# A copy on ScalarE and a normalisation on VectorE change places in the first attention branch of a fused two-block transformer kernel

## The reference

```python
sc = jnp.einsum('bhcqd,bhckd->bhcqk', qblk, kt).astype(jnp.float32) * scale
p = jax.nn.softmax(sc, axis=-1)
w = p[:, :, 0] - lam * p[:, :, 1]
return jnp.einsum('bhqk,bhkd->bhqd', w.astype(vt.dtype), vt)
...
oa = (rms_norm(oa, subln_g_a[l]) * (1.0 - lam_init)).reshape(b, s, WIDTH_A)
```

## Time and profile before

| what | value |
|---|---|
| three runs | 4124.42, 4115.85, 4124.31 us |
| the profiled execution | 4120.0 us, span 4118.3 us |
| mean granted TensorE clock | 0.953 |
| PE, DVE, ACT busy | 89%, 64%, 38% of the span |
| branch A, layer 0 | 157 to 441 us of the span |
| branch A, layer 1 | 1243 to 1514 us of the span |

### The profile page before, as it was taken

How to read it: one execution, slowest core, us unless ns; L and a number is a source line. 1 busy time by engine, 2 the same in 40 slices (tenths; PEclk the granted TensorE clock), 3 DMA queues, 4 the chain that set the end, 5 groups by cost and what they waited for, 6 DMA issues and landing times. The chain is left out here.

```text
span 4118.3 us, 50129 instructions
## 1 busy us (share of the span) xinstructions
PE 3655.4 (89%) x17647; PEld 3038.4 (74%) x17647; DVE 2632.1 (64%) x5013; ACT 1553.7 (38%) x2760; POOL 607.0 (15%) x508
## 2 busy tenths in 40 slices
PE   3887899999888888998997988987887999999998
PEld 2656787788766677777785845667887888888887
DVE  6766424577666653247775655559996767777777
ACT  3344434332234443433223433432286333333332
POOL 2100000101030000011011200043300223322222
PEclk8999999999999999999998988999998999999999
DMA  6332122355221112224451200022346788888887
GB/s 245 108 96 67 35 77 82 114 192 207 79 82 42 54 31 67 72 86 160 175 202 64 75 6 6 12 95 90 94 177 261 279 306 294 314 294 302 298 307 267
DMA packets 180822, 598.68 MB, mean 145 GB/s; under 512 B 18944, under 2 KB 55552, under 8 KB 177280
## 3 DMA queue, kind: packets, MB, share of 16 engines
q1 hardware_dynamic: 129488, 409.78, 28.1%
q0 software_dynamic: 51120, 186.14, 12.9%
HBM read 559.15 MB, written 36.70 MB: 145 GB/s over the span
## 5 line engine op out<-in xcount | busy, mean ns | idle before, releaser
L389 PE MATMUL ps<-mix_w,mix_h 128*128 128x384 f32 (+1 forms) x2304 | 537.1, 383 | 55.7 <-DVE mix_h L1103 22.7
L3189 PE MATMUL ps<-peer_v,peer_coef 128*128 128x512 f32 x2304 | 544.7, 392 | 26.8 <-DVE peer_coef L3304 15.8
L389 PEld LDWEIGHTS ps<-mix_w,mix_h 128*128 128x128 f32 x2304 | 424.7, 196 | 160.7 <-issue 51.0
L3189 PEld LDWEIGHTS ps<-peer_v,peer_coef 128*128 128x128 f32 x2304 | 431.9, 188 | 116.9 <-issue 16.0
L3178 PE MATMUL ps<-peer_h,peer_u 128*128 128x384 f32 x2208 | 401.1, 336 | 3.7 <-PEq L102 3.7
L3178 PEld LDWEIGHTS ps<-peer_h,peer_u 128*128 128x128 f32 x2208 | 389.0, 188 | 10.9 <-issue 4.0
L1259 PE MATMUL ps<-mlp_coef,mlp_v 128*128 128x512 f32 x1536 | 354.0, 391 | 24.4 <-DVEq L1375 24.4
L1259 PEld LDWEIGHTS ps<-mlp_coef,mlp_v 128*128 128x128 f32 x1536 | 290.3, 189 | 85.7 <-DVEq L1375 25.3
L1248 PE MATMUL ps<-mix_h,mlp_u 128*128 128x512 f32 x1344 | 310.6, 392 | 18.3 <-DVEq L1364 18.3
L1248 PEld LDWEIGHTS ps<-mix_h,mlp_u 128*128 128x128 f32 x1344 | 253.9, 189 | 72.7 <-DVEq L1364 19.5
L823 DVE TENSOR_TENSOR mix_w<-mix_raw,mix_w 128x1024 fp32r<-128x1024 f32 (+1 forms) x136 | 153.3, 1143 | 238.7 <-ACT mix_w L612 238.7
(11 more groups left out here) (553 smaller groups left out, 6551.7 us busy)
## 6 DMA issues: line engine op xcount, KB each, us to landing
peer_raw_v<-in_v_tiles SPq DMA_DIRECT2D x128, 512.0 KB, 10.2
peer_raw_u<-in_u_tiles SPq DMA_DIRECT2D x104, 512.0 KB, 11.6
mlp_tiles<-in_w_ada POOLq DMA_DIRECT2D x96, 512.0 KB, 4.6
mix_raw<-in_w_rest SPq DMA_DIRECT2D x68, 512.0 KB, 3.6
mlp_raw_v<-in_w_down SPq DMA_DIRECT2D x16, 2048.0 KB, 8.1
mlp_raw_u<-in_w_up SPq DMA_DIRECT2D x56, 512.0 KB, 9.3
mix_raw<-in_w_a SPq DMA_DIRECT2D x48, 512.0 KB, 3.7
expert_weights<-peer_table SPq DMA_DIRECT2D x6, 4096.0 KB, 12.3
```

Source lines behind the costliest of these rows:

```text
L389: last = pe.matmul(proj(u, n_cols), M.H[:, x, k, b * P:(b + 1) * P], V.w[:, y, i % SLOTS_W, k % 2 * n_cols:(k % 2 + 1) * n_cols], start=k ...
L3189: last = pe.matmul(bank(M.ps, 2 * b + half), Q.coef[:, x, t % 4, b * P:(b + 1) * P], Q.v[:, y, t % 4, half * BANK:(half + 1) * BANK], star ...
```

## The change

There are three edits. On ScalarE `a_back(n)`, the copy of the transposed weights, moves from the end of the even half to the place directly behind the exponentials, ahead of `a_post`, `unit_root` and `high`. On VectorE `head_norm` moves from the end of the odd half j = 33 + 8h to the end of the next even half, j = 34 + 8h: behind that half's maximum, sums, low parts and rope, and ahead of the next `a_weigh`. In `a_values` TensorE now waits for the output block of the step before to be taken, where it waited for the one four steps before; `a_post(n - 1)`, which itself waits for that block, used to stand ahead of the copy that the values wait for.

```diff
--- before.py
+++ after.py
@@ -447,8 +447,8 @@
             def a_values(n):
 
                 h, b = a_step(n)
-                if n >= 4:
-                    pe.wait_ge(o_taken, n - 3)
+                if n:
+                    pe.wait_ge(o_taken, n)
                 if n % 16 == 0:
                     pe.wait_ge(freed_even, (12 * (n // 16) + 12) // 2)
                     pe.wait_ge(freed_odd, (12 * (n // 16) + 12) // 2)
@@ -763,6 +763,7 @@
                             a_exp(0)
                         if n + 1 < A_STEPS:
                             a_exp(n + 1)
+                        a_back(n)
                     if in_b:
                         m = (j - B_FIRST) // 2
                         if m == 0:
@@ -778,8 +779,6 @@
                 for i in due(j):
                     high(i)
                 if not odd:
-                    if in_a:
-                        a_back(n)
                     if in_b:
                         b_back((j - B_FIRST) // 2)
                 elif j > A_FIRST + 8 and (j - A_FIRST - 9) % 8 == 0 and (j - A_FIRST - 9) // 8 < HEADS_A:
@@ -996,8 +995,8 @@
                     dve.tensor_tensor(V.ob[:, LO, pair], bank(M.ps, 6), V.ob[:, HI, pair], ALU.subtract).then_inc(ob_low, 1)
                 if not odd and j > A_FIRST and (j - A_FIRST - 8) % 8 == 0 and 0 <= (j - A_FIRST - 8) // 8 < HEADS_A:
                     head_mean((j - A_FIRST - 8) // 8)
-                if odd and j > A_FIRST + 8 and (j - A_FIRST - 9) % 8 == 0 and (j - A_FIRST - 9) // 8 < HEADS_A:
-                    head_norm((j - A_FIRST - 9) // 8)
+                if not odd and j > A_FIRST + 9 and (j - A_FIRST - 10) % 8 == 0 and (j - A_FIRST - 10) // 8 < HEADS_A:
+                    head_norm((j - A_FIRST - 10) // 8)
                 if odd and j >= 20 and done < late_sums:
                     late_sum(done)
                     done += 1
```

## The result

The changed kernel took 4125.63 us (median of 20 runs, 4118.88 to 4133.61), the kernel before 4119.18 us on the same chip (20 runs, 4110.15 to 4126.84). The ratio is 1.0016 [1.0008, 1.0023]: 6.4 us slower in the middle, within the 0.2% that the forecast called no change. The forecast of 4126 us was met to 0.4 us, and that is partly luck. The loss was put at 3.2 us and is 6.4, but the kernel before took 4119.18 us in the median of these 20 runs, 5.1 us less than the 4124.31 us that the prediction had at hand.

A forecast was written before the change was run, and what follows sets the result against it. TensorE, 89% busy, sets the pace overall, but VectorE's list ends many branch A steps. A layer wins 11.4, loses 11.9 and 1.1 for the clock: 3.2 us slower in all, 4127.5, set at 4126 us, range 4108 to 4140.

The forecast's parts named there:

- What ends a step: Branch A, maximum to maximum: about 40 of 62 steps end by VectorE's list or roped tile; earlier copy only moves waits.
- TensorE's gaps close: Rival: path through TensorE in every step, so copy waits give back 38 us, 4086; chance 0.28 of over 8.2 faster.
- The copy's delay for root and cast: ScalarE behind the copy: 0.5 us later in ten rope steps (5.0 us a layer) and four cast steps (2.0 us).
- The norm: VectorE, a layer: 8.0 us won in five steps, 3.2 lost in steps 5 and 21, 0.3 in 9, 17, 25.
- The term for step 12: Step 12 loses the norm, but TensorE is next: about 0.4 us of 1.6 won, as a mean of the layers.
- "nothing" for step 28: Step 28 already ends on TensorE, so taking the norm away there wins nothing.
- The copy's gain: Values earlier: 0.42 us each in steps 2, 6, 18, 22, 0.2 in 29, 30 (2.1 a layer); 0.9 in 10, 26.
- Step 0: First step of branch A in each layer: two casts begin 1.4 us later behind the copy, 1.4 us lost.
- The clock: Step 22: gathered waiting of over 3 us brings TensorE's low clock, 1.1 us a layer lost; nothing else charged.
- the low clock in the rope steps: Rival: TensorE's longer waits for roped tiles lower the clock, up to 22 us, 4148; slower, with late transposes, chance 0.22.
- The signs: Expected profile after: copy waits about half of 77.7 us, L519 waits up 0.5 per rope step, branch A within 4 us.
- the third rival: The low clock in the rope steps, where roped-tile waits grow to 2 to 3.6 us in five steps; chance 0.22.

The follow-up runs named there:

- e2: Kernel before with only the copy moved directly behind the exponentials, and the new wait of the values: 4139.49 us, ratio 1.0049.
- e7: Kernel before with the copy first only in the ten even-half rope steps of a layer, and the new wait of the values: 4134.46 us, ratio 1.0035.
- e1: Kernel before with only the norm moved, to where the change puts it; copy and wait as before: 4104.01 us, ratio 0.9964.
- e3: Changed kernel with the norm directly behind the maximum, ahead of sums and low parts: 4121.19 us, ratio 1.0003.
- e4: Kernel before with only the norm moved, directly behind the maximum; copy and wait as before: 4102.43 us, ratio 0.9961.
- e5: e4 with the copy first in the 12 steps of a layer without rope, cast or head mean behind it: 4099.19 us, ratio 0.9944.
- e6: e4 with the copy first only in steps 2, 6, 10, 13, 18, 22, 26, 29 and 30: 4107.64 us, ratio 0.9966.
- e8: e4 with three matmuls whose result nobody reads ahead of the values in steps 6 and 22: 4105.39 us, ratio 0.996.
- e10: e5 with three idle matmuls ahead of the values in steps 6, 10, 22 and 26: 4096.35 us, ratio 0.9943.
- e9: Changed kernel with three idle matmuls ahead of the values in steps 11, 22, 27 and three behind them in 11, 27: 4118.29 us, ratio 1.0004.

## Why the prediction was right, and where its terms were off

**What ends a step.** Right. The prediction said that an earlier copy makes TensorE wait somewhere else, and refused to count the 77.7 us. The wait for the copy halved, the wait for rope doubled, from 21.8 to 45.4 us, and a wait for the norm of 13.5 us came up; the rival "TensorE's gaps close", 4086 us, is out.

**The copy's delay for root and cast.** Right in mechanism and size: 0.48 us on ScalarE's queue, 0.5 to 0.6 us in each of steps 3, 7, 15 and 19, and in e2 and e7 the same in 4, 8 and 24.

**The norm.** Right where it was priced: e1 has 1.6 us less in each of five steps, 1.6 us more in steps 5 and 21; the low parts ahead of it were the reason, as e3 and e4 show by taking them away. The term for step 12 and the "nothing" for step 28 were too small. These steps were taken to end on TensorE almost at once, but in e1 step 12 gains 1.5 and 0.7 us and step 28 1.0 and 0.6. In layer 0 half of step 12's gain comes back in step 13, where the prediction had the norm covered: 6.37 us before, 7.16 to 7.19 in the changed kernel, e1, e3, e4, e5, e6, e8 and e10. The prediction's terms give 9.8 us for the norm alone, the runs 15 us (10 to 20, by the ends of the interval times 4119). Part of that is not the norm's: step 26 of layer 1 and step 18 of layer 0 have no norm in them; their old 9.89 and 7.88 us had the low clock in them (scores of 2.08 and 1.93 us, 1.13 in e1).

**The copy's gain.** The short steps won more than 0.42 us: steps 2 and 18 of layer 0 went from 7.83 and 7.88 to 5.93 and 5.81, 1.5 and 1.6 us more than the shift gives. In these the clock was low before and is high now, which the prediction did not count, as it took step 2 of layer 1 (6.36 us) for the pattern: the values of step 2 took 2.07 us before and 1.16 after, behind waits of 2.37 and 2.32 us, and the scores of step 18 took 1.93 and 1.13 us. That is not shown to be the edit's doing: step 18 of layer 0 has fast scores in e1 too, where its copy stands late. Where the clock was high already the rule holds: 6.36 to 5.93, 6.25 to 5.82.

**Step 0.** Right: charged with 1.4 us, and 1.35 us longer in layer 0 and 1.19 in layer 1.

**The clock.** The mechanism was right, and its place too narrow. Step 22 was charged with 1.1 us for the clock, 0.7 with its gain, and is 1.2 us longer; at the upper level it takes 5.82 us (e9), so that the clock costs 1.6 us there. Step 6, which paid before, is no worse after. What was put among the rivals, the low clock in the rope steps, came in six of the twenty: 11 and 27 in both layers, 23 and 24 in layer 0, each 0.6 to 1.3 us beyond the prediction's own terms, 5.9 us together. (In steps 4 and 20 the scores were slow as well, but VectorE was later still.) Six was the number at which the prediction put the loss over 0.2%, so the condition of this rival was met. What kept the time at 6.4 us all the same were the gains in steps 2, 6, 18 and 29, 4.4 us above their term. These were not foreseen, and so the prediction has luck in it here too. Of the table's other rows step 22 is 1.0 us above its term, the last row 1.8, and steps 10, 12, 26 and 28 are 1.5 us below; the rest adds about 1 us. The last row is step 13 of layer 0, named above, and step 25, which takes 0.3 and 1.2 us more in the changed kernel, and 0.1 to 1.0 us in e9, but has its old length in every other run; no run tells why. Together they carry the branches from 3.6 us, twice the table's 1.8, to 7.5.

The Trainium skill, "TensorE: Matmul & The Clock Gate", section "Why this matters for your kernels", asks to leave no idle gaps between bursts of matmuls. The traces agree in the main: after 3.86 us of standing still the clock was 0.50 in step 27, and after 2.74 us it was 0.54 in e4's step 22, where in the kernel before waits of 1.37 and 1.54 us were followed by scores of 1.13 us. The last section has waits that do not fit.

**Two errors that cancelled.** The sum for the two parts was near, 3.2 against 6.4 us, because both parts were too small, each by a little more than its interval leaves open: the norm's gain was put at 9.8 us and measured 15, the copy's loss at 13.0 (the sum without the norm's terms, 6.5 a layer) and measured 20 (14 to 27). A reader should take the net from a sum like this with more care than its steps.

**The signs.** As predicted: 77.7 to 39.8 us ("about half"); step 4 of layer 1 at 9.94 (9.8); step 5 +2.08 (2.1); step 3 +0.57 (half); the wait for the cast 2.88 to 3.37 us; the clock of the branch within 0.02. Not as predicted: the waits of L519 rose by 1.2 us a step, not 0.5, since the values come earlier too (this stood in the third rival alone); the values of step 5 come 3.56 and 4.01 us after the maximum, and those of step 21 4.1 and 4.2, for there TensorE is still busy with the tiles of L389 when the copy is done; and the branch grew by 4.5 us in layer 0, a little over the 4 (3.0 in layer 1).

**What stays open.** That a filled step does not show in the runs of e8 and e10 as it does in their timelines. The steps that lengthened in exchange (10, 26, 27 in e8) have slow scores, of 1.81 to 2.08 us, but whether a step pays differs from one execution to the next by as much as an edit, as the pairs in the last section show. One profile of each kernel does not settle it. Whether a copy in two halves would cost the root less was not tried.

## What to carry to other kernels

Where three engines wait for each other in a ring, the wait of the busiest engine is the wrong number: find for each step which queue's list ends it, and price an edit by what stands behind it in that queue. An instruction that is moved forward helps in the steps that its own result ends and costs most of its length (0.5 of 0.58 us here) in those ended by what it overtook, so move it only where nothing waits behind it (e5), and put work that was in front of an end into a place where its engine waits anyway (e1, e4). Look then at the waits that are left. In a step that TensorE ends they can cost a second time, in the clock: step 22 took 5.8 to 6.3 us with fast scores and 7.4 to 8.4 with slow ones. In a step that another engine ends slow scores cost nothing (step 21, 12.10 us before and in e8, with scores of 2.08 and 1.13 us).

## What the hardware showed that was not expected

Matmuls whose result nobody reads can shorten a step: in e8 six instructions that fill 2.73 us of a wait shorten the step behind them from 8.43 to 6.25 us, since the four scores take 1.13 us at a clock of 1.00 and 2.08 us at 0.54. The runs of e8 as a whole show no gain from it. The same scores took 1.99 us in step 22 and 2.08 us in step 27 of the changed kernel.

The low clock is not tied to a step, nor to the length of the one wait in front of it. In step 2 of layer 0 a wait of 2.37 us left the values at the lower level before (2.07 us) and one of 2.32 us at the upper after (1.16 us). In step 26 of layer 1 values and scores took 2.08 us each behind a wait of 2.76 us before, and 1.16 and 1.13 us behind one of 2.74 us in e1. Step 18 of layer 0 took 7.88 us before and 6.25 in e1. In neither of these steps was anything edited in e1.
